# Loading three weight chunks of a mixture-of-experts stream as 112 rows plus twice eight rows

## The reference

```python
def swiglu(h, w_gate, w_up, w_down):
    return (jax.nn.silu(h @ w_gate) * (h @ w_up)) @ w_down

def moe_swiglu(h, w_router, w_gate, w_up, w_down):
    ...
    for e in range(N_EXPERTS):          # 8 experts, hidden width 3584
        out = out + combine[:, e:e + 1] * swiglu(t, w_gate[e], w_up[e], w_down[e])
```

## Time and profile before

| | us |
|---|---|
| median of three runs | 1144.1 (1142.36 to 1144.64) |
| profiled execution, device time | 1142.71 |
| its span (first to last instruction) | 1140.9 |
| TensorE (PE) busy | 1123.9 (99%) |
| DMA, hardware queue q1 | 83.5% of 16 engines over the span |
| granted TensorE clock, mean | 0.998 |

### The profile page before, as it was taken

One profiled execution on the slowest core, in us unless ns is written; L12 is line 12 of the kernel. 1 busy time (PEld: TensorE's weight loads), 2 busy tenths in 40 slices (PEclk: granted clock), 3 DMA queues, 4 the chain that ended last, 5 costly groups with the idle time before them and its releaser, 6 DMA issues.

```text
span 1140.9 us, 14902 instructions
## 1 busy us (share of the span) xinstructions
PE 1123.9 (99%) x6247; PEld 497.1 (44%) x6248; DVE 312.3 (27%) x561; ACT 136.8 (12%) x293; POOL 17.2 (2%) x58
## 2 busy tenths in 40 slices
PE   9999999999999999999999999999999989999996
PEld 7645566764553334343333334333333423333332
DVE  3556865666541111110201011020101101110102
ACT  1452011110131100000101000010100001110001
POOL 2300000000000000000000000000000000000000
PEclk9999999999999999999999999999999999999999
DMA  7535333447298999999999999999999999999994
GB/s 298 221 119 213 148 147 113 190 177 302 106 432 359 401 402 425 433 430 428 428 431 432 430 427 431 429 429 430 431 429 429 429 432 427 428 431 427 429 425 196
DMA packets 19702, 402.92 MB, mean 353 GB/s; under 512 B 3360, under 2 KB 3360, under 8 KB 4256
## 3 DMA queue, kind: packets, MB, share of 16 engines
q1 hardware_dynamic: 19616, 401.67, 83.5%
HBM read 400.61 MB, written 1.05 MB: 352 GB/s over the span
## 4 chain that ended last, share of the span: by engine, by line
PE 91%; DMA 7%; DVE 1%; ACT 0%; issue 0%; SPq 0%; DVEq 0%; ACTq 0%
PE bank L1789 33%; PE bank L1919 14%; PE bank L1521 12%; PE bank L1760 9%; PE bank L1556 6%; DMA ring<-moe_w_up 4%; DMA ring<-moe_w_down 3%; PE bank L1950 2%; PE bank L1468 2%; PE bank L1851 2%; PE bank L1412 2%; PE bank L1720 1%; PE bank L1743 1%; PE bank L1702 1%; DMA ring<-attn_w_qkv 1%; PE bank L1379 1%
## 5 line engine op out<-in xcount | busy, mean ns | idle before, releaser
L1789 PE MATMUL bank<-ring,arena 128*64 128x448 f32 x2048 | 393.3, 542 | 3.1 <-DMA ring<-moe_w_up 2.3
L1789 PEld LDWEIGHTS bank<-ring,arena 128*64 128x64 f32 x2048 | 145.0, 137 | 249.1 <-issue 244.1
L1919 PE MATMUL bank<-ring,arena 128*64 128x512 f32 x896 | 198.7, 595 | 1.2 <-DMA ring<-moe_w_down 1.0
L1521 PE MATMUL bank<-ring 128*128 128x384 f32 (+1 forms) x448 | 134.4, 459 | 0.0
L1919 PEld LDWEIGHTS bank<-ring,arena 128*64 128x64 f32 x896 | 62.1, 137 | 123.1 <-issue 120.0
L1248 DVE TENSOR_TENSOR arena<-bank,arena 128x448 f32<-128x448 f32 x32 | 20.0, 624 | 331.3 <-PE bank L1789 331.3
L1521 PEld LDWEIGHTS bank<-ring 128*128 128x128 f32 x448 | 84.3, 190 | 45.8 <-issue 0.5
L1760 PE MATMUL bank<-ring,arena 128*32 128x448 f32 x1024 | 99.7, 541 | 0.0
L1760 PEld LDWEIGHTS bank<-ring,arena 128*32 128x32 f32 x1024 | 31.5, 110 | 64.4 <-issue 64.4
L918 DVE TENSOR_TENSOR ring<-ring 128x1536 f32<-128x1536 f32 (+2 forms) x35 | 53.2, 1540 | 10.3 <-PE bank L1455 9.3
L762 ACT ACTIVATE arena<-bank 128x448 f32<-128x448 f32 x32 | 17.4, 543 | 283.6 <-PE bank L1789 283.4
(11 more groups left out here) (217 smaller groups left out, 683.8 us busy)
## 6 DMA issues: line engine op xcount, KB each, us to landing
ring<-moe_w_gate SPq DMA_DIRECT2D x31, 3584.0 KB, 21.9
ring<-moe_w_up SPq DMA_DIRECT2D x31, 3584.0 KB, 26.1
ring<-moe_w_down SPq DMA_DIRECT2D x29, 3584.0 KB, 25.1
ring<-ffn_w_gate SPq DMA_DIRECT2D x3, 3072.0 KB, 10.1
ring<-ffn_w_up SPq DMA_DIRECT2D x3, 3072.0 KB, 10.1
ring<-ffn_w_down SPq DMA_DIRECT2D x3, 3072.0 KB, 10.0
ring<-moe_w_down SPq DMA_DIRECT2D x3, 2048.0 KB, 31.0
ring<-moe_w_down SPq DMA_DIRECT2D x3, 1536.0 KB, 34.2
```

The costliest lines, as they stand in the source:

```text
L1521: last = mm(ffn_bank(m, i), b[lhs][:, k, :], b[rhs][:, k, :], start=k == 0, stop=k == 3)
L1789: last = mm(bank[2 * (j % 2) + up][64 * h:64 * h + 64, 0:FJ], xg[:, k, side:side + BASE], w[:, k, h, :], start=k == 0, stop=k == KD - 1)
L1919: last = mm(bank[2][64 * h:64 * h + 64, :], hg[:, i0 + i, half * BASE:half * BASE + BASE], w[:, i, h * BANK:h * BANK + BANK], start=d == 0 ...
```

## The change

For chunks (2, 3), (4, 3) and (6, 3) the one transfer of 128 rows becomes three: rows 0 to 111 in one, counted on `full` as before, then rows 112 to 119 and rows 120 to 127, counted on a new semaphore for each of the three chunks. TensorE waits for that semaphore too before it reads the chunk. Bytes, order of the chunks and buffers stay the same.

```diff
+ROW_GROUP = 8
...
+        last_rows = [sem(f"last_rows{n}") for n in range(3)]
...
+        def in_rows(it, c):
+
+            return {(2, 3): 0, (4, 3): 1, (6, 3): 2}.get((it, c)) if isinstance(it, int) else None
...
+                elif in_rows(it, c) is not None:
+                    at = P - 2 * ROW_GROUP
+                    sp.dma_start(ring[s][0:at, :], w[0:at, :]).then_inc(full[s], 16)
+                    for r in range(at, P, ROW_GROUP):
+                        sp.dma_start(ring[s][r:r + ROW_GROUP, :], w[r:r + ROW_GROUP, :]
+                                     ).then_inc(last_rows[in_rows(it, c)], 16)
...
+                    if in_rows(it, c) is not None:
+                        pe.wait_ge(last_rows[in_rows(it, c)], 32)
```

## The result

The changed kernel takes 1202.6 us (median of six runs, 1200.7 to 1205.8) against 1144.4 us before in the same measurement; the ratio is 1.0522, 95% interval 1.0509 to 1.0535. One of the six runs before took 1976.9 us and is left out of the ratio. Slower, as forecast, but by 58 us where 21 were forecast, and outside the stated range, which ended at 1180. The profiled execution has a span of 1204.1 us against 1140.9, so 63.2 us are to be found between the two traces.

A forecast was written before the change was run, and what follows sets the result against it. The landing of the last weights through a full DMA stream sets the end; 22.5 us for three chunks less 2.7 of lead, plus 1.7 of slow clock, is 21.5 us: about 1165 us, range 1140.9 (rounded down) to 1180.

The forecast's parts named there:

- The end is set by the landing of the last weights, and the whole delay of the stream is a delay of the end: At the last chunk, PE already waits 1.0 us for weights, so stream delay, halfway 19.8 us, reaches the end in full.
- Two more issues and one more wait are free: On SyncE, two extra 0.33 us issues a chunk are hidden; on PE, one wait of some tens of ns: zero.
- The 112 rows: 7.5 us in place of 8.56: At each changed chunk, sixteen engines take seven rows each, 7.5 us instead of 8.56, if rows are dealt out evenly.
- Eight-row transfers: four row times each: At each changed chunk, each small transfer takes 4.3 us, eight rows through two ways; a row time is 1.07 us.
- Only the engines that carry the small transfers pay, 15 row times in place of 8: At each changed chunk, the engines with small transfers need 7.5 us more, three times 22.5 us.
- A lead of the early engines: In the weight stream, engines without instruction fetches may be up to 5.4 us ahead; halfway, 2.7 us comes off the loss.
- One more 1.7 us of slow clock: On PE before the last chunk, a longer wait can make the next matmuls run at the lower clock: 1.7 us.
- Rival 1: In the stream, parallel small transfers move rows off late engines: -3.2 to 0 us, 1141.9 us; chance 0.30.
- rival 2: In the stream, parallel small transfers fall on engines not ahead: last landing 3.2 us later, 1147.3 us; chance 0.12.
- The signs by which I wanted to know it: Rate dips after 540, 747, 954 us; last small transfer some 9 us after 112 rows; waits at (6, 0), (6, 1) over 10.

The follow-up runs named there:

- the control: Against the kernel before: the three chunks each in three transfers of all 128 rows, cut by columns (7/8, 1/16, 1/16), same extra issues and wait; 1143.4 us, ratio 1.0001.

## Why the prediction went wrong, point by point

- *The end is set by the landing of the last weights, and the whole delay of the stream is a delay of the end.* Right: the change at (2, 3) alone loses 14 us in its dip and 16 us at the end.
- *Two more issues and one more wait are free.* Right: the control is at 1.0001.
- *The 112 rows: 7.5 us in place of 8.56, "if the rows are dealt out evenly".* This step failed, and it is the largest. Alone, with an eighth of the bytes gone, these transfers cost 38 us. I had bounded them "from the good side" only. Everything I argued about eight neighbours (the full rate is seen only where all 128 partitions are written) held for 112 rows as well, and I didn't apply it.
- *Eight-row transfers: four row times each.* About right in size: alone they come out at +2.7 us with 7.5 us of rows a chunk left out, and the rate goes to 115 of 430 GB/s, a quarter. In part that is luck, since the slowness isn't confined to the engines that carry them.
- *Only the engines that carry the small transfers pay, 15 row times in place of 8.* Failed. All sixteen slow down together, those in the chunk before or after too. 64 + 64 rows show it in its simplest form: 23 us at half rate for a chunk that is 17 us long at that rate.
- *A lead of the early engines is used up first and takes 2.7 us off.* Not borne out. The lead is larger than I had worked out, 9.6 us at the last weights and not 5.4, but it hid nothing: the dip lasts longer where the stream is further on, 40 us against 28.
- *One more 1.7 us of slow clock.* The mechanism was right, the size not: PE's matmuls take 14.9 us more in all, since there are many waits and not one.
- *Rival 1, work moved from late engines to early ones.* Falls, and not only for the neighbours: with rows four apart it is +13 us. Leaving out half a chunk for the other eight engines gave 1 us; after (6, 3) PE's only wait is one of 1.0 us, so there was hardly more to win. The packed traces also bear on rival 2. Without rows 64 to 127 the two last engines are done with (6, 4) at 963.0 and 963.1, and in the kernel before the last one is done at 963.2. So two of the latest engines are among the eight that the small transfers use, which is the condition of that rival.

The signs by which I wanted to know it did their work in part. The dips are there, at 530, 747 and 966 us. The last small transfer landed 1.0, 5.2 and 5.8 us after the 112 rows and not 9: the 112 rows were slow themselves. PE's waits grew to over 10 us, but not where I had said. I expected them at (6, 0) and (6, 1); the longest are at the changed chunks themselves, since the three changed chunks hold the stream down for some 28, 37 and 49 us and not for the 16 that I had summed.

## What to carry to other kernels

A load whose rows don't span the partitions in the way of the rest of the stream isn't a smaller load but a disturbance of all transfers in flight: give every transfer of a full stream all 128 partitions, and cut by columns where it must be cut, which cost nothing here. When a step has no row in the trace, bound it from both sides, and apply one argument to every part of the change for which its premise holds. To see such a thing, read the rate in windows of 2 us: a share of 1.00 of the engines hides it.

## What the runs showed of the hardware

- The rate of all sixteen engines is halved while eight-row transfers bring rows 64 to 127, every fourth (251, 194 GB/s), and is down to a quarter with two transfers of eight neighbouring rows (115 GB/s, rows of 3.0 to 3.9 us in place of 1.07). It falls within one to two microseconds for all. What couples the engines that touch none of these rows no run has shown.
- Rows 0 to 63, every fourth, in eight-row transfers run at full rate (413, 437 GB/s); this fits that the eight engines that such transfers use are those that bring these rows in the 128-row transfers too.
- SyncE needs more time to issue a transfer of rows four apart. SPq in order of time, sixteen transfers of neighbouring rows and then sixteen of rows four apart:

```profile
916.28 7.28 SPq L487 DMA_DIRECT2D ring<-moe_w_up  x16
```

```profile
916.68 13.93 SPq L488 DMA_DIRECT2D ring<-moe_w_up  x16
```

0.46 us each against 0.87 us.
